# Two experts' outputs added by TensorE with one-hot gates, and the residual not lent as a place for weights, in a two-layer decoder trunk

## The chip, the cores and the metric

One core of one Trainium2 chip. The time is that of the whole program in device microseconds (us), the median of several executions. The profile is taken from one more execution.

## What is computed

Input x is 512 tokens of width D = 1024 in float32. Two layers, each of a token mixer (layer 0: RWKV-7 time mixing, layer 1: a Conformer convolution module) and a mixture of 32 gated-MLP experts of which each token uses two, with a residual around each, and a root-mean-square norm ahead of each and at the end:

```python
for i in range(2):
    hn = rms_norm(h, norm1_g[i])
    h = h + (rwkv7_time_mix(hn) if i == 0 else conformer_conv(hn))
    hn = rms_norm(h, norm2_g[i])
    # router: top 1 of 4 groups, top 2 of its 8 experts; ge is zero but for two experts of a token
    y = 0
    for wg, wu, wd, ge in experts:                 # (1024,256), (1024,256), (256,1024)
        y = y + ge[:, None] * ((silu(hn @ wg) * (hn @ wu)) @ wd)
    h = h + y
return rms_norm(h, final_g)
```

## The kernel before

All 512 tokens lie in four tiles of 128 partitions; h, the residual, is 128 x 4096 float32 in SBUF (2 MB). Each engine has a program of its own, written out by hand; they meet only at semaphores. The stages are: mixer 0, norm and routing, experts of layer 0, load back and combination, mixer 1, norm and routing, experts of layer 1, load back and combination, final norm.

**Experts.** Routing gives each expert up to 64 slots. In `pe_moe`, for each expert, TensorE multiplies the gathered rows of a pair of experts (`columns`, L911, then `gate_up`, L944), turns the product (`flip`, L920) and multiplies by the second matrix (`down`, L957). ScalarE applies silu (L987), copies the turned product (L993) and the result (`take_y`, L998) to SBUF; VectorE weighs (L1015) and gates (L1030). GpSimd gathers rows of the residual from DRAM (`rows`, L862) and scatters each result to the tensor `chosen` in DRAM (L871), four rows of 512 per token: two choices, two halves. After the last result is in DRAM (`round_done`), `act_load_back` reads `chosen` back, 1 MB a tile, and `dve_combine` (L1065) adds it to h with the gate of each token, two additions a tile.

**Weights.** SyncE (SP) issues all weight loads in one queue, in order: 2 MB of gate and up (`sp_load_up`, L404, in two halves L392 for some) and 1 MB of down (L409) for each expert. The up matrices have RING = 7 places, the down matrices DOWN_RING = 7. `sp_moe_weights` loads expert e into the place of expert e - 7 once that has been multiplied. Six of the up places are memory of their own; the seventh is h itself: once the normed rows are made and the residual has been stored to `rows` in DRAM (L847), `sp_load_into_h` loads expert 6 there, and after expert 27 `sp_return_h` (L422) reads the residual back.

**Around the experts.** `pe_stay_busy` (L740) issues matmuls whose result nobody uses. `pe_ranks`, `pe_slots` (L797) and `pe_factors` (L808) count slots and put row factors in slot order; `dve_tables` makes the index tables. All of this runs once ahead of the loop over rounds and once more in it for the next round; with this input one round is run. `pe_conv` begins with eight more unused matmuls (L2283), started by the first combined tile; then come transposes of the normed rows (L526) and the first products of the convolution module (L2290). In the norm ahead of it ScalarE squares (L468) and takes logarithm and exponential for two tiles together (`act_norm_rows`), and VectorE multiplies by the factor and by the norm's weights (L498). VectorE's first gate of the module is L2440.

## Time and profile before

| | us |
|---|---|
| median of 3 runs | 1242.36 (1239.82 to 1242.53) |
| the profiled execution | 1240.7 |
| its span in the profile | 1238.9 |
| TensorE busy | 1128.2 (91%) |
| VectorE busy | 521.1 (42%) |
| ScalarE busy | 419.4 (34%) |
| GpSimd busy | 214.3 (17%) |

The first mixer and the routing last until about 520 us, layer 0's experts until 738, the convolution module and its routing until about 991, layer 1's experts until 1209, the rest until the end. The page cuts the span into 40 slices of 31 us. Matmuls in float32 are listed as two passes each, so that a matmul of 512 columns counts as two; a busy TensorE is not one at its peak.

### The profile page before, as it was taken

The numbers are of one execution on the slowest core, as the hardware profiler recorded it, in microseconds if no ns is written. First come the engines' busy times: TensorE is split into PE (matmuls) and PEld (weight loads), VectorE is DVE, ScalarE is ACT, GpSimd is POOL, SyncE is SP. The second block draws the span as 40 slices with busy tenths as digits, with TensorE's granted clock in tenths as the row PEclk, the third lists the DMA queues.
The fourth block names the chain that finished last, engine by engine and source line by source line (L and its number), as shares of the span: only waits on it lengthen the run. The fifth ranks groups of instructions, "written<-read, shape, count | busy, mean of one in ns | idle before, by whom it ended". The sixth has DMA issues, their size and how long they took to land.

```text
span 1238.9 us, 29223 instructions
## 1 busy us (share of the span) xinstructions
PE 1128.2 (91%) x12462; PEld 622.5 (50%) x12462; DVE 521.1 (42%) x964; ACT 419.4 (34%) x815; POOL 214.3 (17%) x245
## 2 busy tenths in 40 slices
PE   6999999999999999899998876999999899998880
PEld 5455555555555644555554434544554455554440
DVE  5756555564665411511110105799941511111105
ACT  5335445444454421311111113555443321111112
POOL 2000000000000000222221110688800222222110
PEclk9999999999999989899998987999999899999995
DMA  4011101011012168799999996216502899999996
GB/s 159 3 54 62 40 21 58 4 57 41 20 58 85 59 248 332 258 406 423 426 423 426 425 385 252 93 68 249 244 0 74 318 352 423 425 425 424 425 381 240
DMA packets 51923, 274.57 MB, mean 222 GB/s; under 512 B 14900, under 2 KB 17076, under 8 KB 34642
## 3 DMA queue, kind: packets, MB, share of 16 engines
q1 hardware_dynamic: 39184, 243.28, 48.9%
q0 software_dynamic: 10880, 21.00, 4.5%
q10 hardware_dynamic: 1728, 8.42, 1.8%
q8 instruction: 100, 1.64, 0.5%
q14 instruction: 31, 0.24, 0.1%
HBM read 266.36 MB, written 23.07 MB: 234 GB/s over the span
## 4 chain that ended last, share of the span: by engine, by line
PE 78%; DMA 11%; ACT 4%; DVE 3%; issue 2%; SPq 2%; ACTq 0%; POOLq 0%; DVEq 0%
PE psum L944 14%; PE psum L1504 14%; PE psum L2034 9%; PE psum L2312 8%; DMA big<-in_moe_w_gate_up_dram 7%; PE psum L957 7%; PE psum L1685 6%; DMA big<-in_moe_w_down_dram 2%; PE psum L911 2%; PE psum L1808 1%; PE psum L2322 1%; PE psum L2290 1%; PE psum L526 1%; PE psum L1834 1%; ACT big L1867 1%
## 5 line engine op out<-in xcount | busy, mean ns | idle before, releaser
L944 PE MATMUL psum<-big 128*64 128x256 f32 x1536 | 191.6, 393 | 21.2 <-issue 12.9
L1504 PE MATMUL psum<-big 128*128 128x512 f32 x384 | 191.0, 618 | 5.5 <-ACT big L1555 4.3
L944 PEld LDWEIGHTS psum<-big 128*64 128x64 f32 x1536 | 107.2, 139 | 89.2 <-issue 30.6
L1030 DVE SCALAR_TENSOR_TENSOR big<-psum,big 128x128 f32<-128x128 f32 x64 | 22.5, 351 | 304.9 <-ACT big L987 304.9
L957 PE MATMUL psum<-big 128*64 128x512 f32 x512 | 120.9, 593 | 2.1 <-DMA big<-in_moe_w_down_dram 1.5
L871 POOL DMA_INDIRECT chosen<-big x64 | 63.7, 996 | 330.3 <-ACT big L998 177.2
L2034 PE MATMUL psum<-big 128*128 128x512 f32 x256 | 116.3, 607 | 0.8 <-ACT big L2417 0.8
L1877 ACT COPY big<-psum 128x512 f32<-128x512 f32 (+1 forms) x112 | 68.4, 649 | 113.6 <-PE psum L1685 111.7
L2262 POOL TENSOR_TENSOR big<-big 128x512 f32<-128x512 f32 x76 | 96.7, 1273 | 34.3 <-ACT big L2399 24.1
L847 POOL DMA_DIRECT2D rows<-h x8 | 4.7, 582 | 555.6 <-DVE h L2073 555.6
L2312 PE MATMUL psum<-big,conv_w 128*128 128x512 f32 x224 | 96.5, 592 | 0.0
L1504 PEld LDWEIGHTS psum<-big 128*128 128x128 f32 x384 | 64.8, 189 | 59.9 <-issue 53.9
L1685 PEld LDWEIGHTS psum<-big 64*64 64x64 f32 x4096 | 70.5, 134 | 43.0 <-issue 43.0
L2473 DVE SCALAR_TENSOR_TENSOR psum<-big,conv_taps,psum 128x512 f32<-128x512 f32 x123 | 82.3, 750 | 0.0
L1685 PE MATMUL psum<-big 64*64 64x64 f32 (+1 forms) x4096 | 80.0, 227 | 0.3 <-ACT big L1877 0.2
L2034 PEld LDWEIGHTS psum<-big 128*128 128x128 f32 x256 | 48.3, 194 | 58.4 <-issue 54.6
L2399 ACT ACTIVATE big<-big,conv_taps 128x512 f32<-128x512 f32 x84 | 57.2, 716 | 46.5 <-DVE big L2440 28.4
L993 ACT COPY big<-psum 128x128 f32<-128x128 f32 x64 | 17.0, 265 | 155.3 <-PE psum L920 106.7
L2312 PEld LDWEIGHTS psum<-big,conv_w 128*128 128x128 f32 x224 | 42.6, 190 | 53.1 <-issue 53.1
L998 ACT COPY big<-psum 128x512 f32<-128x512 f32 x64 | 37.4, 585 | 88.6 <-PE psum L957 88.6
L1015 DVE TENSOR_TENSOR big<-psum,big 128x1024 f32<-128x1024 f32 (+1 forms) x34 | 39.3, 1161 | 65.3 <-PE psum L911 65.3
L957 PEld LDWEIGHTS psum<-big 128*64 128x64 f32 x512 | 36.6, 137 | 48.1 <-issue 37.5
(273 smaller groups left out, 1355.9 us busy)
## 6 DMA issues: line engine op xcount, KB each, us to landing
big<-in_moe_w_gate_up_dram SPq DMA_DIRECT2D x40, 2048.0 KB
big<-in_moe_w_down_dram SPq DMA_DIRECT2D x64, 1024.0 KB
conv_w<-in_moe_w_gate_up_dram SPq DMA_DIRECT2D x8, 2048.0 KB
h<-in_moe_w_gate_up_dram SPq DMA_DIRECT2D x8, 2048.0 KB
big<-in_moe_w_gate_up_dram SPq DMA_DIRECT2D x16, 1024.0 KB, 38.4
big<-in_rwkv_w_rkv_dram SPq DMA_DIRECT2D x24, 512.0 KB, 4.3
conv_w<-in_conv_w_pw_dram SPq DMA_DIRECT2D x8, 1024.0 KB, 4.8
big<-chosen ACTq DMA_DIRECT2D x6, 1024.0 KB, 9.3
```

The lines of the kernel that those rows point to most:

```text
L871: nc.gpsimd.indirect_dma_start(chosen[m.layer], bass.IndirectOffsetOnAxis(ap=m.scatter_at[:, e:e + 1].bitcast(u32), axis=0), m.y[e % Y_RIN ...
L944: last = nc.tensor.matmul(o[half * SLOTS:(half + 1) * SLOTS, 0:F_EXP].rearrange("p (u f) -> p u f", u=2), m.xT[e // 2 % 2][:, c, (e % 2) * ...
L957: last = nc.tensor.matmul(bank[6 + e % 2][half * SLOTS:(half + 1) * SLOTS, :], m.zT[e % 2][:, k, :], m.down[j][:, k, half * 512:(half + 1) ...
L1015: return nc.vector.tensor_tensor(m.xT[p % 2][:, first:end, :], psum[:, first * P:end * P].rearrange("p (c s) -> p c s", s=P), m.g_col[:, f ...
L1504: last = nc.tensor.matmul(bank[b], m.w[:, n, c, :], x[:, c, :], start=(c == 0), stop=(c == C - 1))
L1685: last = nc.tensor.matmul(bank[b + hd][half(par ^ (hd & crossed)), at:at + w.shape[1]], lhs(hd, cp, par), w, start=True, stop=True)
L1877: nc.scalar.copy(dst, src).then_inc(done.now(), 1)
L2034: return nc.tensor.matmul(bank[4 * (t % 2) + nh], src[:, c, t * P:(t + 1) * P], wts[:, nh * 512:(nh + 1) * 512], start=(c == 0), stop=(c = ...
L2262: nc.gpsimd.tensor_tensor(out_, m.product[n % 4], m.product[(n - 1) % 4] if k == 1 else out_, ALU.add).then_inc(m.pool_tap, 1)
L2312: last = nc.tensor.matmul(up_bank(q, u), m.w1[b][:, c, u, :], m.hnT[:, c, :], start=(c == 0), stop=(c == C - 1))
L2399: nc.scalar.activation(m.product[n % 4], m.u[b][:, at:at + T], ACT.Copy, scale=m.taps[:, q, at:at + 1]).then_inc(m.product_ready, 1)
L2473: done[k % 2] = st.done(nc.vector.scalar_tensor_tensor(out=m.co[:, q, :] if k == DVE_TAPS[q] - 1 else acc[k % 2], in0=m.u[b][:, k:k + T], ...
```

## The change

**Two experts not scattered.** The results of experts 30 and 31 are no longer written to `chosen`. VectorE makes, for each of the two, a matrix of 128 tokens by slots with the gate in it (`spread_gates`); TensorE turns it (`turn_hot`), ScalarE copies it to SBUF (`take_hot`), and behind the last `down` TensorE multiplies it by the result: 64 slots x 128 tokens times 64 x 512, two halves, two experts, four tiles (`add_last`). VectorE adds these sums from PSUM to h. The gates of the other rows are set to zero where the row belongs to expert 30 or 31.

**The load back** waits for expert 29's scatter alone (`round_done` is raised there), is issued by SP at the end of `sp_moe_weights` and lands in the up places 2 and 3. The combination is now inside the round, in the order COMBINE, with `dve_tables` for the next round behind the second addition.

**The residual stays in SBUF.** RING is 6; `sp_load_into_h` and `sp_return_h` are gone. `chosen` has rows that nobody writes, so it is filled once with finite values (`sp_finite`, eight DMAs of 1 MB behind the convolution vectors' load in the first mixer).

**Norms behind the experts.** Tile by tile: ScalarE squares, takes logarithm and exponential and writes the scaled rows. For the convolution module the norm's weights are applied at the transposed columns, by ScalarE in eight copies a tile (tiles 0 and 1) or by VectorE in two (tiles 2 and 3). In the final norm GpSimd multiplies tiles 0 and 1 by the weights and VectorE makes tiles 2 and 3. The eight unused matmuls of `pe_conv` and one of three ahead of the experts are gone; `pe_factors` moves into the loop. `pe_slots` of the next round moves from expert 28 to expert 31.

```diff
-RING = 7
+RING = 6
 DOWN_RING = 7
 N_PAIRS = N_EXP // 2
 Y_RING = 2
+ADDED_BY_PE = 2
+SCATTERED = N_EXP - ADDED_BY_PE
...
-                self.back = [big[:, stage_base // 2 + 2 * D * t:stage_base // 2 + 2 * D * (t + 1)] for t in range(TT)]
+                places = [ring_up[n].rearrange("p u c f -> p (u c f)") for n in (2, 3)]
+                self.back = [places[t // 2][:, t % 2 * 2 * D:(t % 2 + 1) * 2 * D] for t in range(TT)]
...
-        def sp_load_into_h(m, sp):
-
-            sp.wait_ge(m.squares.sem, m.squares.by(TT))
-            sp.wait_ge(m.hnT_in_psum.sem, m.hnT_in_psum.by(TT))
-            sp.wait_ge(m.rows_stored.sem, m.rows_stored.by(16 * TT))
-            sp_load_up(m, sp, RING - 1)
-
-        def sp_return_h(m, sp, rounds):
-
-            assert max(range(RING - 1, N_EXP, RING)) <= LAST - FREE2
-            sp.wait_ge(m.gate_up_done, FREE2 - 2 + UPS_A_ROUND * rounds)
-            sp.dma_start(h, rows[m.layer].rearrange("(t p) d -> p t d", p=P)).then_inc(m.first_pick_in, 16)
-
...
+            sp_load_back(m, sp, 0)
...
+        def sp_load_back(m, sp, r):
+
+            back = chosen[m.layer].rearrange("(t p c) n -> t p (c n)", p=P, c=4)
+            sp.wait_ge(m.round_done, r + 2)
+            sp.dma_start(m.back[0][:, 0:D], back[0][:, 0:D]).then_inc(m.first_pick_in, 16)
+            sp.dma_start(m.back[0][:, D:], back[0][:, D:]).then_inc(m.back_in[0].sem, 16)
+            for t in range(1, TT):
+                sp.dma_start(m.back[t], back[t]).then_inc(m.back_in[t].sem, 16)
+
+
+
+        COMBINE = tuple(("pick", t, k) for t in range(2) for k in range(2)) + tuple(
+            ("last", t, n) for t in range(2) for n in range(2)) + tuple(
+            (what, t, n) for t in range(2, TT) for what in ("pick", "last") for n in range(2))
+        H_STEPS = len(COMBINE)
+
+        def h_step_of(what, t, n):
+            return COMBINE.index((what, t, n)) + 1
...
+        def act_norm_root(m, act, rounds, t):
+
+            act.wait_ge(moe[m.after].h_step, summed(moe[m.after], rounds, t))
+            nc.scalar.activation(big[:, last_region:last_region + D], h[:, t, :], ACT.Square,
+                                 accum_out=m.ss[:, t:t + 1]).then_inc(m.squares.sem, 1)
+            rstd = m.rstd[:, t:t + 1]
+            act.wait_ge(m.squares.sem, m.squares.by(t + 1))
+            nc.scalar.activation(rstd, m.ss[:, t:t + 1], ACT.Ln, scale=1.0 / D, bias=rms_eps[:]).then_inc(m.rstd_step.sem, 1)
+            act.wait_ge(m.rstd_step.sem, m.rstd_step.by(2 * t + 1))
             nc.scalar.activation(rstd, rstd, ACT.Exp, scale=-0.5).then_inc(m.rstd_step.sem, 1)
...
+        def act_norm_rows(m, act, t):
+
+            act.wait_ge(m.rstd_step.sem, m.rstd_step.by(2 * t + 2))
+            if t >= len(m.hn):
+                act.wait_ge(m.hnT_in_psum.sem, m.hnT_in_psum.by(t - len(m.hn) + 1))
+            nc.scalar.activation(m.hn[t % len(m.hn)], h[:, t, :], ACT.Copy, scale=m.rstd[:, t:t + 1]
+                                 ).then_inc(m.hn_ready.sem, 1)
...
+                for e in range(SCATTERED):
+                    if e + 1 < SCATTERED:
                         scatter(e + 1)
                     if e % 2 == 0 and e // 2 + 4 < N_PAIRS:
                         gather(e // 2 + 4)
                     scattered(e)
                 pool.sem_inc(m.round_done, 1)
+                pool.wait_ge(m.last_added.sem, TT * r + (m.last_added.before + TT))
+                pool.sem_inc(m.y_free, ADDED_BY_PE)
...
+        GATES_A_ROUND = ADDED_BY_PE * TT + 2
...
-            pe_stay_busy(m, 3)
+            pe_stay_busy(m, 2)
             rounds = load_rounds(m, pe)
             with pe.Fori(0, rounds) as r:
+                pe.wait_ge(m.h_step, H_STEPS * r + H_STEPS)
+                pe_factors(m, pe, r)
...
+                def turn_hot(j):
+
+                    pe.wait_ge(m.last_hot_ready.sem, ADDED_BY_PE * r + (m.last_hot_ready.before + j + 1))
+                    pe.wait_ge(m.xT_ready, ROWS_A_ROUND * r + (FREE1 + rows_of(N_PAIRS - 1)))
+                    for t in range(TT):
+                        last = nc.tensor.transpose(bank[j][:, t * P:(t + 1) * P], m.last_hot[:, t, :], ident[:])
+                    last.then_inc(m.last_turned.sem, 1)
+
+                def add_last(j, t):
+
+                    for half in range(2):
+                        s = slice(half * SLOTS, (half + 1) * SLOTS)
+                        last = nc.tensor.matmul(bank[LAST_BANKS[t][half]], m.last_rows[s, j, t * P:(t + 1) * P],
+                                                m.y[(SCATTERED + j) % Y_RING][s, :], start=(j == 0),
+                                                stop=(j == ADDED_BY_PE - 1))
+                    return last
...
+                    if e == LAST:
                         pe.wait_ge(m.slot_step, TABLE_STEPS * r + TABLE_STEPS)
+                        pe.wait_ge(m.factor_ready.sem, r + (m.factor_ready.before + 1))
                         pe.sem_inc(pe_tick)
                         pe_slots(m, pe, r + 1)
                     if e % 2 == 0 and e + 2 < N_EXP:
                         columns(e // 2 + 1)
+                    if e in (LAST - 2, LAST - 1):
+                        turn_hot(e - (LAST - 2))
                     if e + 1 < N_EXP:
                         gate_up(e + 1)
                     else:
                         flip(e)
                     down(e)
...
+                rows_turned(0)
+                add_last(0, 1)
+                rows_turned(1)
+                add_last(0, 0)
+                add_last(1, 0).then_inc(m.last_added.sem, 1)
+                add_last(1, 1).then_inc(m.last_added.sem, 1)
+                add_last(0, 2)
+                add_last(1, 2).then_inc(m.last_added.sem, 1)
+                pe.wait_ge(m.h_step, H_STEPS * r + (H_STEPS + h_step_of("last", 1, 1)))
+                add_last(0, 3)
+                add_last(1, 3).then_inc(m.last_added.sem, 1)
+            return rounds
...
+                def take_hot(j):
+                    act.wait_ge(m.xT_in_psum, ROWS_A_ROUND * r + rows_of(N_PAIRS - 2))
+                    act.wait_ge(m.last_turned.sem, ADDED_BY_PE * r + (m.last_turned.before + j + 1))
+                    nc.scalar.copy(m.last_rows[:, j, :], bank[j]).then_inc(m.last_rows_ready.sem, 1)
+
...
+                def spread_gates(j):
+
+                    dve.wait_ge(m.hot_ready, TT * 2 * r + TT * 2)
+                    if j:
+                        dve.wait_ge(m.last_turned.sem, ADDED_BY_PE * r + (m.last_turned.before + j))
+                    for t in range(TT):
+                        nc.vector.tensor_scalar(m.last_hot[:, t, :], m.hot[:, 2 * t, :], m.last_gate[:, t, 0, j:j + 1], None,
+                                                ALU.mult).then_inc(m.gates_step.sem, 1)
+                    for t in range(TT):
+                        dve.wait_ge(m.gates_step.sem, GATES_A_ROUND * r + (m.gates_step.before + TT * j + t + 1))
+                        last = nc.vector.scalar_tensor_tensor(out=m.last_hot[:, t, :], in0=m.hot[:, 2 * t + 1, :],
+                                                              scalar=m.last_gate[:, t, 1, j:j + 1], in1=m.last_hot[:, t, :],
+                                                              op0=ALU.mult, op1=ALU.add)
+                    last.then_inc(m.last_hot_ready.sem, 1)
...
+                def combine(what, t, n):
+
+                    if n or what == "last":
+                        dve.wait_ge(m.h_step, H_STEPS * r + (H_STEPS + h_step_of(*(("pick", t, n - 1) if what == "pick" and n
+                                                                                   else ("pick", t, 1)))))
+                    if what == "pick":
+                        if t == 0 and n == 0:
+                            dve.wait_ge(m.first_pick_in, 16 * r + 16)
+                        else:
+                            dve.wait_ge(m.back_in[t].sem, 16 * r + (m.back_in[t].before + 16))
+                        nc.vector.scalar_tensor_tensor(out=h[:, t, :], in0=m.back[t][:, n * D:(n + 1) * D],
+                                                       scalar=m.gate_now[:, n, t:t + 1], in1=h[:, t, :], op0=ALU.mult,
+                                                       op1=ALU.add).then_inc(m.h_step, 1)
+                    else:
+                        dve.wait_ge(m.last_added.sem, TT * r + (m.last_added.before + t + 1))
+                        part = h[:, t, n * 512:(n + 1) * 512]
+                        nc.vector.tensor_tensor(part, bank[LAST_BANKS[t][n]], part, ALU.add).then_inc(m.h_step, 1)
...
+                    if e == LAST - 4:
+                        spread_gates(0)
+                    if e == LAST - 2:
+                        spread_gates(1)
+                    if e == LAST - 1:
+                        dve.wait_ge(m.last_hot_ready.sem, ADDED_BY_PE * r + (m.last_hot_ready.before + ADDED_BY_PE))
+                        dve_slots(m, dve)
+                        gates_of_round()
+                for step in COMBINE:
+                    combine(*step)
+                    if step == ("pick", 0, 1):
+                        dve_tables(m, dve, r + 1)
             return rounds
-
-        def act_load_back(m, act, rounds):
...
-            pe.wait_ge(moe[0].h_step, 2)
-            for _ in range(8):
-                nc.tensor.matmul(bank[1], ident[:], h[:, 0, 0:512], start=True, stop=True)
...
+            def columns(t):
+                act.wait_ge(m.hnT_in_psum.sem, m.hnT_in_psum.by(t + 1))
+                for c in range(C):
+                    last = nc.scalar.activation(m.hnT[:, c, t * P:(t + 1) * P],
+                                                bank[NORM_BANKS[t % 2][c // 4]][:, c % 4 * P:(c % 4 + 1) * P], ACT.Copy,
+                                                scale=m.g_col[:, c:c + 1])
+                    if c % 4 == 3:
+                        last.then_inc(m.hnT_ready.sem, 1)
...
+        def dve_conv(m, dve):
+            dve.wait_ge(m.vec_in, CONV_VECTORS_IN)
+            for t in range(2, TT):
+                dve.wait_ge(m.hnT_in_psum.sem, m.hnT_in_psum.by(t + 1))
+                for half in range(2):
+                    c = slice(4 * half, 4 * half + 4)
+                    nc.vector.tensor_tensor(m.hnT[:, c, t * P:(t + 1) * P],
+                                            bank[NORM_BANKS[t % 2][half]].rearrange("p (c t) -> p c t", t=P),
+                                            m.g_col[:, c].unsqueeze(2).broadcast_to([P, 4, P]), ALU.mult
...
+        def sp_finite(sp):
+
+            for m in moe:
+                rows_of_tokens = chosen[m.layer].rearrange("(t p k c) n -> t p k (c n)", p=P, k=2, c=2)
+                for t in range(TT):
+                    sp.dma_start(rows_of_tokens[t], h[:, t, :].unsqueeze(1).broadcast_to([P, 2, D])
+                                   ).then_inc(chosen_finite.sem, 16)
+
+        def pool_final(m, pool):
+            pool.wait_ge(m.params_in.sem, m.params_in.by(16))
+            for t in range(EARLY):
+                pool.wait_ge(m.hn_ready.sem, m.hn_ready.by(t + 1))
+                nc.gpsimd.tensor_tensor(m.hn[t], m.hn[t], m.g_row, ALU.mult).then_inc(m.early_rows.sem, 1)
```

## Rows read from the trace of the kernel before

**Rows 1.** Page, part 2: granted clock of TensorE and GB/s in 40 slices of the span.

```profile
PEclk9999999999999989899998987999999899999995
...
GB/s 159 3 54 62 40 21 58 4 57 41 20 58 85 59 248 332 258 406 423 426 423 426 425 385 252 93 68 249 244 0 74 318 352 423 425 425 424 425 381 240
```

**Rows 2.** Waits of TensorE, 655:738, then 1105:1209: total us, times, longest us.

```profile
PE psum L944 <- issue: 8.5, 4, 2.6
PE psum L944 <- DMA big<-in_moe_w_gate_up_dram: 2.7, 3, 1.9
...
PE psum L957 <- DMA big<-in_moe_w_down_dram: 1.5, 2, 0.9
```

**Rows 3.** Timeline of SyncE's DMA issues, layer 0: start us, us, engine, line, operation.

```profile
509.66 0.33 SPq L404 DMA_DIRECT2D h<-in_moe_w_gate_up_dram  x1
522.29 7.38 SPq L392 DMA_DIRECT2D big<-in_moe_w_gate_up_dram  x4
...
718.01 0.38 SPq L422 DMA_DIRECT2D h<-rows  x1
```

**Rows 4.** Windows, layer 0's experts: us, busy by engine, PEclk, DMA share, GB/s.

```profile
522.30:735.60 213.30, 200.12 (x1424) 107.44 (x1420) 31.08 (x55) 39.56 (x96) 43.41 (x43) 0.98 1.01 417
```

**Rows 5.** Timeline behind layer 0's experts, columns as in rows 3, idle before it in brackets.

```profile
730.70 0.98 POOL L871 DMA_INDIRECT chosen<-big  x1 [8.55 <-ACT big L998]
...
735.65 1.94 PE L957 MATMUL psum<-big 128*64 128x512 f32 x8 [0.59 <-ACT big L993]
...
749.57 2.70 DVE L1065 SCALAR_TENSOR_TENSOR h<-big,h 128x1024 f32<-128x1024 f32 x2 [2.24 <-DMA big<-chosen]
...
764.94 3.72 PE L2290 MATMUL psum<-big,conv_w 128*128 128x256 f32 x16 [1.25 <-ACT big L480]
...
781.03 0.75 DVE L2440 SCALAR_TENSOR_TENSOR big<-psum,conv_vec,big 128x512 f32<-128x512 f32 x1 [11.72 <-PE psum L2290]
```

**Rows 6.** The chain that ended last, behind layer 0's experts: start us, us, what.

```profile
739.07 6.18 DMA chosen<-big
```

**Rows 7.** Timeline behind layer 1's experts.

```profile
1200.50 0.98 POOL L871 DMA_INDIRECT chosen<-big  x1 [6.58 <-ACT big L998]
...
1206.68 1.94 PE L957 MATMUL psum<-big 128*64 128x512 f32 x8 [0.90 <-DMA big<-in_moe_w_down_dram]
...
1217.71 1.28 DVE L1065 SCALAR_TENSOR_TENSOR h<-big,h 128x1024 f32<-128x1024 f32 x1 [2.12 <-DMA big<-chosen]
...
1233.29 2.61 DVE L498 SCALAR_TENSOR_TENSOR big<-h,big 128x1024 f32<-128x1024 f32 x2 [0.51 <-ACT big L475]
```

**Rows 8.** Groups by line: xcount | busy us, mean ns | idle before it.

```profile
L2262 POOL TENSOR_TENSOR big<-big 128x512 f32<-128x512 f32 x76 | 96.7, 1273 | 34.3 <-ACT big L2399 24.1 <-POOL big L2262 0.4
...
L1065 DVE SCALAR_TENSOR_TENSOR h<-big,h 128x1024 f32<-128x1024 f32 x16 | 20.5, 1284 | 8.0 <-DMA big<-chosen 7.2
...
L993 ACT COPY big<-psum 128x128 f32<-128x128 f32 x64 | 17.0, 265 | 155.3 <-PE psum L920 106.7 <-issue 48.6
...
L1981 DVE TENSOR_TENSOR big<-big 128x256 f32<-128x256 f32 x8 | 3.3, 416 | 0.0
...
L688 DVE TENSOR_TENSOR big<-big,token_high 128x256 bf16<-128x256 f32 x4 | 2.4, 630 | 0.1
...
L2455 DVE TENSOR_TENSOR big<-psum,big 128x512 f32<-128x512 f32 x3 | 2.1, 692 | 0.4 <-PE psum L2322 0.3
```

**Rows 9.** Timeline of layer 0's routing: GpSimd beside VectorE's L688.

```profile
507.75 2.10 POOL L831 TENSOR_TENSOR big<-big 128x256 bf16<-128x256 f32 x3 [6.17 <-DVE big L683]
```

**Rows 10.** Timeline of TensorE: eight passes in the first mixer, six passes of filling.

```profile
119.81 3.67 PE L1504 MATMUL psum<-big 128*128 128x512 f32 x8 [0.61 <-ACT big L1555]
...
513.37 5.30 PE L740 MATMUL psum<-big,ident 128*128 128x512 f32 x6
```

**Rows 11.** Timeline of TensorE (first mixer), and a window of the output's writes.

```profile
143.97 1.12 PE L1504 MATMUL psum<-big 128*128 128x512 f32 x2
...
1236.00:1237.00 1.00, 0.00 (x0) 0.00 (x0) 0.00 (x0) 0.00 (x0) 0.00 (x0) 0.50 0.93 381
```

255 lines of the change are left out of this document (112 added, 143 removed).

## The prediction

> **What bounds the kernel now.** The slices of the page come first [rows 1]. In both mixture-of-experts stages (slices 17 to 22 and 33 to 37) the core's DMA moves 423 to 426 GB/s, whatever else is going on. To see which of the two sets the pace, read the waits of TensorE over the last 83 us of layer 0's experts [rows 2]: 8.5 us in four gaps that the view can only call issue, and 2.7 us that it gives to gate and up weights. Over the first 130 us the same view is empty. So TensorE runs ahead of the weights at first, uses up what was loaded in advance, and from 655 us it goes at the pace of the weight stream. Layer 1 ends the same way [rows 2]. In that regime the end of the experts is the end of the stream: what was not in SBUF when the stream began has to be moved at 417 GB/s [rows 4].
>
> Behind the last expert nothing of that sort holds. Layer 0: last `down` begins at 735.65 and takes 1.96, so it ends at 737.6; the output goes to SBUF, is scattered to DRAM from 739.07 on [rows 6], read back, and VectorE's first gated addition is at 749.57, 12.0 us after the last matmul; the mixer's first gate is at 781.03 [rows 5]. Layer 1: 1208.6, 1217.71 (9.1 us), last row of the final norm 1233.29 for two of 1.3, end at 1238.9 [rows 7]. The tails are therefore 43.4 and 30.3 us long. The profiled execution took 1240.7 us, 1.7 under the median of the runs.
>
> **What the change does to the weight stream.** The seventh `up` place was the residual's own 2 MB. Its load for expert 6 is issued at 509.66 and has 12.6 us to itself before the first place comes free, at 522.29 [rows 3]; it fills time in which nothing else of the stream is to be moved. With RING = 6 these 2.1 MB wait for expert 0 to free its place, and are moved inside the saturated stretch: 2.10 MB by 417 GB/s is 5.0 us, per layer [rows 4]. The 2 MB read that returned the residual (issued 718.01) goes, but it was queued after the last weight, so it gives nothing back to them. In the new order `down` 7 is issued behind both halves of `up` 8 (the places for `up` 6 to 8 come free in the first 13 us, at the rate at which experts finish), and by then the queue runs dry once for 0 to 2 us: I take 0.9. Moving `pe_slots` (16 short matmuls, about 0.64 us) to just before the last `flip` delays the last `down` by 0 to 0.6: 0.3, since that `down` mostly waits for its weights. The two hot-matrix transposes (half a microsecond of TensorE each), 16 small VectorE operations in `spread_gates` and two 128x512 copies on ScalarE lie in the last four experts, where each engine waits for the stream anyway: nothing; were the stream not the limit they would cost at most 1 us on TensorE. Sum: **+6.2 us a layer, +12.4**, bounds 4.9 and 7.6 a layer.
>
> **What it takes from the tails.** The load back no longer waits for the last scatter but for that of expert 29. That one was issued at 730.70 and 1200.50, 6.9 and 8.1 us before the last matmul ended [rows 5, 7]. The last scatter took 6.2 us in layer 0 with the DMA still loaded [rows 6], and so ended at 745.3. With 6 to 7 us for it, round_done comes about when the last `down` ends, 0.6 us before or after; issue to first addition is 4.3 us (745.3 to 749.57). So the first addition is at **+3.5 us** after the last matmul instead of 12.0 and 9.1. Bounds 2.5 and 5.5. SP is blocked on round_done there; queued behind it are the mixer's first weights, issued at 718.4 before, which now follow 4 MB of read-back: 5 MB, 12 us, still before their use.
>
> **What it puts there instead.** VectorE had eight additions of 1.28 us; it now has the eight, eight of 128x512 from PSUM at 0.69 and the tables of the next round (five small operations, about 1.1 us by an estimate from the 0.4 of a 256-wide one and less) in between [rows 8]: 17.8 us from first addition to last, in the order of COMBINE: rows of tile 0 complete at 8.2 (2.7 before), tile 1 at 9.6, tile 2 at 13.7, tile 3 at 17.8. TensorE's 16 products are 32 passes of 512 columns; even one behind the other at 0.46 us [rows 10] those of tile 0 are done 6 us after the last `down`, of tile 1 8 us and of tile 2 11 us, and VectorE asks for them at 10.2 us and later.
>
> Layer 0, counted from the first addition: ScalarE does square, logarithm, exponential and scaled copy of a tile in 2.9 us (two passes over 1024 columns at about a microsecond and two single columns at 0.2, my estimate), so the rows are normed at 11.1 and 14.0. Its eight small copies for a tile's columns are 2.1 us (0.265 each [rows 8]); columns of both tiles at 18.1 (before: TensorE begins its products at 764.94, which is 15.4). Then 256-wide products: four groups of 3.5 us at full clock. They follow, with the transposes of tiles 2 and 3 (ScalarE delivers at 20.8 and 23.6) and VectorE's scaled copies between, to 35.0 at full clock. The change also takes out the eight dummy matmuls (L2283) that kept TensorE busy from the end of the first tile on and brought the clock up before these products. The granted clock of the slice with that tail is 0.7 in the mean, of the last slice 0.5 [rows 1]; what the lower level costs is seen at the start of the experts, where six filling passes take 5.30 us, 0.88 each, against 0.46 for a pass of the same width at full clock [rows 10]. The first group here would then take 6.9 us, of which 1.7 isn't covered by ScalarE. I take it: first gate at 37.0, against 31.5 before. Tail 3.5 + 37.0 = 40.5 against 43.4: **-2.9 us**.
>
> Layer 1: last addition at 17.8, square, logarithm and exponential of tile 3 to 19.6, its scaled copy on VectorE to 20.9, then the 3.0 us to the end as before: 23.9. New beside it are two 128x1024 multiplications on GpSimd, 2.5 us each by the 1.27 for 512 columns [rows 8], at about 11 and 14 us, when VectorE does additions whose two inputs are both in SBUF. The one place in the trace where both do that at once is L688 beside L831: 0.63 us, where the same width alone takes 0.42 (L1981), half as much again [rows 8, 9]. On the four additions of 1.28 this is 2.5 us: I take that; bounds 0 and 5.1, two whole multiplications. Tail 3.5 + 23.9 + 2.5 = 29.9 against 30.3: **-0.4 us**.
>
> The Trainium skill, "SBUF — State Buffer", section "SBUF: two separate sides", says that the port pair shared by VectorE and GpSimd is an exclusive lock held for the whole instruction. By that rule the price is the upper bound, 5.1 us. The 0.63 against 0.42 speaks for some blocking and can't tell how much of it.
>
> **Starts of the experts and the rest.** TensorE's first transposes follow right behind the six passes of filling, which end at 518.7 [rows 10]. With one filler less and `pe_factors` behind them it could begin up to 1.4 us earlier, once the gather has landed; but the clock may then rise later, up to 2 us lost. I take 0, bounds -1.4 and +2 a layer. The new fill of `chosen` is 8.4 MB of writes issued around 103 us. Output rows are written at 381 GB/s, so it ends near 126 us; the value weights queued behind it are used first at 143.97 [rows 11]. Cost 0; it begins to cost if the writes run under about 220 GB/s.
>
> **Sum.** +12.4 - 2.9 - 0.4 = +9.1 us: 1240.7 becomes 1249.8; I say 1250.
>
> **The rivals.**
> 1. The seventh place was worth nothing: the stream carries 2 MB less (the returned residual) and 2 MB more, and if the DMA engines work on the return and the last weights together, the end doesn't move. It decides at whether the return slowed the last weights by as much as 5 us. For it: the return is issued 16 us before the last `down` ends. Against: it is behind them in the same queue. Then +9.1 - 11.8 = -2.7: 1238, faster. 0.17.
> 2. The tails are as short as they can be: clock full, no loss beside GpSimd, start 0.9 us earlier in both layers: 9.1 - 1.7 - 2.5 - 1.8 = +3.1, with the dry spell gone +1.3: 1242 to 1244, within the limit of what can be told. 0.15.
> 3. GpSimd holds up VectorE for both its multiplications: +2.6 more, 1252.4. The rule cited above says so. 0.18.
> 4. Expert 29's scatter lands late, since it shares engines with the last weights: the first addition at 8 us in both layers, as though nothing had been cut in layer 1: +9, 1259. 0.06.
> The forecast itself: 0.44.
>
> **How the numbers follow.** 0.2% is 2.5 us, about what a measurement of this kernel can tell from none. Faster is rival 1 (0.17), same is rival 2 (0.15), slower the rest, 0.68. The range goes from the middle of rival 1 past rival 3, as far as the bounds of the first addition (2.5 to 5.5, twice) and of the starts reach together: 1238 to 1257.
>
> **What would show it.** The sum of TensorE's waits for weights in the experts rises by about 5 us a layer and the first such wait comes earlier; last `down` to last `down` of layer 0 is the plainest number. First addition 3.5 us after it. Mixer's first gate 40.5 after it, and the end of the span 29.9 after that of layer 1. VectorE's additions longer than 1.28 only in layer 1 after tile 1. I am wrong if the last `down` of layer 0 ends within 2 us of 737.6, or if the load back is issued well before the last `down` ends.

## The result, and the profile after

| | before | after |
|---|---|---|
| median, us | 1241.5 (1239.8 to 1242.5, 4 runs) | 1254.7 (1253.3 to 1255.8, 4 runs) |
| ratio of the runs, with its interval | 1 | 1.0102 [1.0082, 1.0123] |
| span of the profiled execution, us | 1238.9 | 1253.2 |
| mean granted clock of TensorE | 0.967 | 0.974 |

The change costs 13.2 us. I had said 1250, +9.1. The sign and the order of size are right, the size is 4 us short, and that is more than the runs scatter. Medians are of the fast runs alone: e2, e6, e12 and the repeats of before had one run each that took 1642, 1902, 4591 and 2267 us, and it is left out. The changed kernel was timed four times, the experiments at other times beside new runs of before, whose median was then 1242.0 to 1242.7. The ratios are not quite the quotients of two medians. By their intervals, a difference between an experiment and the changed kernel is good to 3 to 4 us; where it is smaller, the time alone doesn't show it. The page of the changed kernel, part 2, has the two rows that answer [rows 1]:

```profile
PEclk9999999999999999899999997999999899999997
...
GB/s 157 3 53 300 61 28 58 5 55 41 19 57 118 25 289 330 184 407 423 422 423 423 422 303 268 68 100 266 187 0 117 229 389 421 423 422 422 422 309 218
```

The fourth slice is new (300 GB/s where there were 62: the fill of `chosen`); the experts run at 421 to 423, before at 423 to 426. To see where the 14.3 us of span went, cut the program at five points that every variant has: the first bf16 matmul of the ranks (routing), the start of ScalarE's copy of expert 31's output (the last `down` has ended), the mixer's first gate, and the same in layer 1. All kernels of this study are cut here, in us; the stretch from the first gate to layer 1's routing was 197.8 to 197.9 in every one, and is left out.

| kernel | routing 0 at | routing to last `down`, layer 0 | tail 0 | routing to last `down`, layer 1 | tail 1 | span |
|---|---|---|---|---|---|---|
| before | 507.8 | 229.9 | 43.4 | 229.8 | 30.3 | 1238.9 |
| after | 508.5 | 238.5 | 40.1 | 237.6 | 30.7 | 1253.2 |
| e1 six places | 507.4 | 235.1 | 40.1 | 236.5 | 29.7 | 1246.6 |
| e2 lend | 511.0 | 235.1 | 40.3 | 235.1 | 32.8 | 1252.1 |
| e3 no GpSimd | 506.7 | 237.7 | 40.5 | 237.2 | 28.5 | 1248.5 |
| e4 warm | 508.3 | 236.6 | 38.5 | 239.0 | 31.0 | 1251.2 |
| e5 before, fill | 509.3 | 232.8 | 43.4 | 229.7 | 30.3 | 1243.4 |
| e6 six, return | 505.5 | 234.7 | 43.2 | 234.5 | 30.3 | 1246.0 |
| e7 combination | 507.6 | 232.5 | 39.4 | 230.6 | 29.8 | 1237.7 |
| e8 aligned | 509.1 | 237.3 | 38.3 | 233.9 | 31.7 | 1248.1 |
| e9 fill in pieces | 507.5 | 238.9 | 40.1 | 236.7 | 30.6 | 1251.7 |
| e10 combination, split | 506.9 | 233.8 | 38.8 | 230.8 | 28.9 | 1237.0 |
| e11 four fillers | 507.9 | 231.4 | 40.4 | 232.3 | 29.6 | 1239.4 |
| e12 before, shifted | 507.7 | 232.0 | 44.2 | 232.3 | 30.4 | 1244.4 |

Before to after: +0.7 (routing), +8.6, -3.3, +7.8, +0.4: together 14.3 with rounding. One execution stands behind each row of the table, and one stretch varies by up to 2 us and more between kernels that are alike in it: before and e5 have 229.8 and 229.7 in layer 1, but e1 and e6, which differ only behind the last weights, have 236.5 and 234.5 there, and routing of the kernels without a fill at once begins at 505.5 to 507.9. A single difference of less than 2 us in this table shows nothing by itself; the rows of the trace that explain it, or several kernels on each side, have to.

The waits of TensorE in layer 0's experts, first 522 to 650, then 650 to 747 (before, the first stretch was empty, and the second is [rows 2]):

```profile
PE psum L940 <- DMA big<-in_moe_w_gate_up_dram: 2.9, 2, 2.2
...
PE psum L940 <- DMA big<-in_moe_w_gate_up_dram: 8.8, 5, 2.5
PE psum L940 <- issue: 3.9, 2, 2.0
PE psum L940 <- DMA conv_w<-in_moe_w_gate_up_dram: 2.0, 1, 2.0
```

[rows 2] leave out one line of the same view of before, the wait for the expert in the lent place:

```profile
PE psum L944 <- DMA h<-in_moe_w_gate_up_dram: 1.4, 1, 1.4
```

With it the waits for gate and up weights were 12.6 us (8.5, 2.7, 1.4). They are 17.6 now, 5.0 more, and they begin before 650. SyncE's issues, and the start of the experts on TensorE, answer to [rows 3, 10]:

```profile
524.42 13.16 SPq L395 DMA_DIRECT2D big<-in_moe_w_gate_up_dram  x6
537.63 0.62 SPq L412 DMA_DIRECT2D big<-in_moe_w_down_dram  x1
...
512.36 1.96 PE L726 MATMUL psum<-h,ident 128*128 128x512 f32 x4
...
518.63 1.97 PE L907 MATMUL psum<-ident,big 128*128 128x128 f32 x8 [3.72 <-DMA big<-rows,big]
520.70 5.61 PE L940 MATMUL psum<-big 128*64 128x256 f32 x32
```

There is no issue at 509; the first place comes free at 524.42, 2.1 us later. The first transposes begin where they did, at 518.63, but behind 3.7 us of standing still, and the first gate and up products take 5.61 us where they took 3.67 before. The same two places in layer 1, the first freed place in before and after and the first products in after:

```profile
993.25 7.38 SPq L392 DMA_DIRECT2D big<-in_moe_w_gate_up_dram  x4
...
999.44 12.96 SPq L395 DMA_DIRECT2D big<-in_moe_w_gate_up_dram  x6
...
995.88 5.25 PE L940 MATMUL psum<-big 128*64 128x256 f32 x32 [0.51 <-DVE big L1053]
```

The issue at the first freed place cuts the stretch of the experts in two: the start, and the part in which the stream sets the pace. In us, layer 0 and layer 1:

| kernel | routing to first freed place | from there to the end of the last `down` |
|---|---|---|
| before | 14.5, 14.4 | 215.3, 215.4 |
| after | 15.9, 14.5 | 222.5, 223.1 |
| e1 six places | 14.4, 13.4 | 220.7, 223.1 |
| e6 six, return | 14.3, 13.4 | 220.3, 221.1 |
| e2 lend | 17.2, 16.3 | 218.0, 218.8 |
| e8 aligned | 16.4, 13.2 | 220.9, 220.7 |
| e12 before, shifted | 15.0, 15.2 | 217.1, 217.1 |
| e10 combination, split | 17.1, 14.0 | 216.7, 216.8 |
| e11 four fillers | 15.1, 14.6 | 216.3, 217.7 |

Behind the last matmul of layer 0, for [rows 5, 6]:

```profile
737.10 0.66 PE L964 MATMUL psum<-ident,big 128*128 128x128 f32 x4
...
738.65 0.98 POOL L861 DMA_INDIRECT chosen<-big  x1 [6.23 <-DMA chosen<-big]
...
741.96 1.94 PE L953 MATMUL psum<-big 128*64 128x512 f32 x8 [0.18 <-DMA big<-in_moe_w_down_dram]
...
743.83 0.64 PE L785 MATMUL psum<-big 128*128 128x64 bf16 x16
...
744.93 0.33 SPq L460 DMA_DIRECT2D big<-chosen  x1
...
746.95 0.58 ACT L1029 COPY big<-psum 128x512 f32<-128x512 f32 x1 [2.04 <-PE psum L953]
...
749.04 1.28 DVE L1106 SCALAR_TENSOR_TENSOR h<-big,h 128x1024 f32<-128x1024 f32 x1 [6.47 <-DMA big<-chosen]
...
768.37 6.39 PE L2356 MATMUL psum<-big,conv_w 128*128 128x256 f32 x16 [3.63 <-ACT big L2442]
...
787.04 0.75 DVE L2518 SCALAR_TENSOR_TENSOR big<-psum,conv_vec,big 128x512 f32<-128x512 f32 x1 [8.80 <-PE psum L2356]
...
738.65 6.14 DMA chosen<-big
```

The load back is issued 2.0 us before the last `down` ends (746.95), and the first addition comes 2.1 us behind it; the mixer's first gate is 38.0 after that. Layer 1, for [rows 7]:

```profile
1222.50 0.58 ACT L1029 COPY big<-psum 128x512 f32<-128x512 f32 x1 [2.13 <-PE psum L953]
...
1224.85 2.72 DVE L1106 SCALAR_TENSOR_TENSOR h<-big,h 128x1024 f32<-128x1024 f32 x2 [6.96 <-DMA big<-chosen]
...
1236.69 1.29 DVE L1112 TENSOR_TENSOR h<-psum,h 128x512 f32<-128x512 f32 x2
...
1237.90 4.56 DVE L1106 SCALAR_TENSOR_TENSOR h<-big,h 128x1024 f32<-128x1024 f32 x2
1238.29 6.37 POOL L2628 TENSOR_TENSOR big<-big 128x1024 f32<-128x1024 f32 x2 [23.33 <-PE psum L971]
...
1242.58 1.29 DVE L1112 TENSOR_TENSOR h<-psum,h 128x512 f32<-128x512 f32 x2
1243.79 3.16 DVE L2641 SCALAR_TENSOR_TENSOR big<-h,big 128x1024 f32<-128x1024 f32 x2
```

### The profile page after: what moved, and what is told of

Its sections match the earlier page's. It is cut to its first block, busy times and chain, and to the rows that moved or that the text cites. A ratio compares the mean times of both kernels' runs of the same rounds, so it can differ in the third digit from the quotient of the medians.

```text
span 1253.2 us, 29408 instructions
## 1 busy us (share of the span) xinstructions
PE 1139.9 (91%) x12474; PEld 626.5 (50%) x12474; DVE 536.0 (43%) x1012; ACT 430.6 (34%) x841; POOL 216.9 (17%) x244
## 4 chain that ended last, share of the span: by engine, by line
PE 67%; DMA 22%; ACT 4%; DVE 4%; issue 2%; SPq 0%; DVEq 0%; POOLq 0%; ACTq 0%
DMA big<-in_moe_w_gate_up_dram 19%; PE psum L1563 14%; PE psum L940 10%; PE psum L2093 9%; PE psum L2379 8%; PE psum L1744 6%; PE psum L953 4%; PE psum L2356 1%; PE psum L1867 1%; PE psum L907 1%; PE psum L2389 1%; DMA big<-chosen 1%; PE psum L505 1%; PE psum L1893 1%; DMA chosen<-big 1%
## 5 line engine op out<-in xcount | busy, mean ns | idle before, releaser
L940 PE MATMUL psum<-big 128*64 128x256 f32 x1728 | 220.1, 399 | 34.9 <-DMA big<-in_moe_w_gate_up_dram 26.4
L940 PEld LDWEIGHTS psum<-big 128*64 128x64 f32 x1728 | 121.7, 142 | 116.1 <-DMA big<-in_moe_w_gate_up_dram 34.9
L861 POOL DMA_INDIRECT chosen<-big x60 | 60.0, 999 | 329.0 <-ACT big L1029 161.9
L2331 POOL TENSOR_TENSOR big<-big 128x512 f32<-128x512 f32 x76 | 96.7, 1273 | 38.5 <-ACT big L2478 28.0
L1053 DVE TENSOR_TENSOR big<-psum,big 128x1024 f32<-128x1024 f32 (+1 forms) x34 | 39.4, 1161 | 61.1 <-PE psum L907 61.1
L953 PEld LDWEIGHTS psum<-big 128*64 128x64 f32 x512 | 36.7, 137 | 47.6 <-issue 37.9
```

The costliest lines, as they stand in the source:

```text
L861: nc.gpsimd.indirect_dma_start(chosen[m.layer], bass.IndirectOffsetOnAxis(ap=m.scatter_at[:, e:e + 1].bitcast(u32), axis=0), m.y[e % Y_RIN ...
L940: last = nc.tensor.matmul(o[half * SLOTS:(half + 1) * SLOTS, 0:F_EXP].rearrange("p (u f) -> p u f", u=2), m.xT[e // 2 % 2][:, c, (e % 2) * ...
L953: last = nc.tensor.matmul(bank[6 + e % 2][half * SLOTS:(half + 1) * SLOTS, :], m.zT[e % 2][:, k, :], m.down[j][:, k, half * 512:(half + 1) ...
L1053: return nc.vector.tensor_tensor(m.xT[p % 2][:, first:end, :], psum[:, first * P:end * P].rearrange("p (c s) -> p c s", s=P), m.g_col[:, f ...
L2331: nc.gpsimd.tensor_tensor(out_, m.product[n % 4], m.product[(n - 1) % 4] if k == 1 else out_, ALU.add).then_inc(m.pool_tap, 1)
```

## The experiments

**e1, six places in the kernel before.** The change's `RING = 6` alone.

```diff
-RING = 7
+RING = 6
-            sp_load_into_h(moe[0], sp)        # and for moe[1]
-            sp.dma_start(h, rows[m.layer]...).then_inc(m.first_pick_in, 16)
```

> The kernel before with one edit of the change alone: RING = 6, so the residual's 2 MB are neither lent to expert 6 nor returned; tails, load back and fillers as before. Theory (the seventh place is worth the 2.1 MB it holds ahead of the saturated stream, 6.2 us a layer forecast, 7 to 8 read from the two traces): last down of layer 0 6 to 8 us after the 737.6 of before, whole time +12 to +15, about 1255, so that the rest of the change gives nothing or a little. Rival 1 (what is moved later is paid by the return that goes): last down of layer 0 within 2 us of 737.6, time within 2.5 us of before, and the 14 us come from something else in the change.

1246.9 us (1244.2 to 1250.9, 10 runs), ratio 1.0032 [1.0017, 1.0047]: +4.4, neither the 12 to 15 nor the 0. The last `down` of layer 0 did come late (742.47, +4.8), as the theory wanted. But the first addition is then 9.15 us behind it, not 11.9 as before, and in layer 1 8.25, not 9.1. So part of what the stream loses comes back behind it. In the part that goes at the stream's pace e1 is 5.4 and 7.7 us longer than before.

**e6, the same with the return kept.** One line back into e1: the read of 2 MB over h, though h was never lent.

```diff
+            sp.dma_start(h, rows[m.layer].rearrange("(t p) d -> p t d", p=P)).then_inc(m.first_pick_in, 16)
```

> The six-place version of before with one thing put back: the 2 MB read that returns the residual, at its old place behind the last weights, although the residual was never lent (it reads the same values over themselves). Theory (the return stands between the last weights and the scatters and load back, and its cost falls in the tail, not in the stream): last down of layer 0 within 1 us of 742.5, but the first addition 11 to 12 us behind it instead of 9.15, and the time 2 to 4 us above that of the six-place version (1246.9). Rival: the return is hidden behind the last experts as I predicted (gives nothing back, costs nothing): first addition 9 to 9.5 us behind, same time.

1249.7 us (1248.5 to 1251.6, 3 runs), ratio 1.0071 [1.0051, 1.0091]. That is 2.8 above e1 by the medians and 4.8 by the ratios, so the return costs something. The chain of e1 and then of e6, behind layer 0:

```profile
743.90 3.31 DMA chosen<-big
```

```profile
741.62 6.44 DMA chosen<-big
```

The last scatter lands in 3.31 us where nothing is queued in front of it, and takes 6.44 where the return is ([rows 6]: 6.18 before). First addition 12.15 and 9.03 us behind the last `down`, as before. This is the price of the return: 3.0 us in layer 0, 0.8 in layer 1. Against before, where all else is equal, the seventh place alone is worth 4.8 and 4.7 us in the table, and 5.0 and 5.7 in the part behind the first freed place. e1 has no return but the same experts, and there it comes to 5.2 and 6.7, and 5.4 and 7.7: four readings of one thing, from 4.7 to 7.7. In layer 1 both reach the first freed place 1.0 us sooner than before, with no lent load on its way then.

**e2, the residual lent again in the changed kernel.**

```diff
-RING = 6
+RING = 7
-                places = [... for n in (2, 3)]
+                places = [... for n in (0, 1)]
+            sp_load_into_h(moe[0], sp)        # and for moe[1]
+            sp_return_h(m, sp, 1)             # in front of the load back
```

> The changed kernel with the residual lent to expert 6 again (RING = 7, returned by a 2 MB read behind the last weights, load back into places 0 and 1 instead of 2 and 3), written for one round of slots, which is what this routing needs. All the rest of the change stays: last two experts added by TensorE, early load back, tables inside the additions, no dummies. Theory: takes back the whole ring loss, 12 to 15 us, to about 1240 to 1242, with the first addition still 2 to 4 us behind the last down unless the returned residual comes late. Rival 1: stays within 2.5 us of the changed kernel's 1254.7. Rival: the returned residual, queued behind the last weights, is what the first addition waits for, and 1 to 3 us of the 12 to 15 are lost again there.

1251.1 us (7 runs), ratio 1.0056 [1.0035, 1.0076]. -3.6 (-5.7 by the ratios), not -12 to -15: the theory that the ring makes the whole loss falls. The stretch is 3.3 and 2.5 us shorter than in the changed kernel (4.6 and 4.5 counted from the first transposes, which come 1.2 and 1.9 us later behind routing; the lent load is on its way with the first gather then), and still 5.3 longer than before in both layers, with as many places: 2.6 and 1.9 of it ahead of the first freed place, 2.6 and 3.4 behind it. The first addition is 4.0 us behind the last `down` instead of 2.1 to 2.4, again the return. What remained was to find 5.3 us in each layer that have nothing to do with the ring.

**e4, filling where TensorE stands still.**

```diff
                 pe_factors(m, pe, r)
+                pe_stay_busy(m, 3)
                 add_last(1, 2).then_inc(m.last_added.sem, 1)
+                for _ in range(4):
+                    nc.tensor.matmul(bank[5], ident[:], m.up[1][:, 0, 0:2, :], start=True, stop=True)
+            for _ in range(3):                # pe_conv, ahead of its wait for hnT_ready
+                nc.tensor.matmul(bank[1], ident[:], h[:, 0, 0:512], start=True, stop=True)
```

> The changed kernel with filling passes of TensorE where it idles: three dummy matmuls of 512 columns behind the gate factors at the start of the experts, four behind the products of tile 2 (both layers), three ahead of the mixer's first products. Theory (the first expert and the first product group run at the lower clock because TensorE stood still before them): first gate_up group 3.7 instead of 5.6 us and first product group 3.5 to 4.5 instead of 6.4; time 2 to 5 us under the changed kernel's. Rival (the lower clock comes whatever is put there, or the groups are covered by ScalarE and the weights): within 1.5 us of it, the first gate no earlier.

1250.8 us (1245.1 to 1252.9, 8 runs), ratio 1.0056 [1.0042, 1.0070]: -3.9. The groups went as the theory said:

```profile
518.83 1.16 PE L908 MATMUL psum<-ident,big 128*128 128x128 f32 x8 [1.42 <-DMA big<-rows,big]
520.50 3.67 PE L941 MATMUL psum<-big 128*64 128x256 f32 x32 [0.51 <-DVE big L1056]
...
766.16 3.72 PE L2359 MATMUL psum<-big,conv_w 128*128 128x256 f32 x16 [0.70 <-ACT big L2447]
```

The granted clock over the first group is 0.65 in the changed kernel and 1.00 in e4 (the number in front of the last two):

```profile
520.70:526.31 5.61, 5.61 (x33) 3.21 (x33) 0.63 (x1) 0.00 (x0) 0.99 (x1) 0.65 0.26 65
...
520.50:524.17 3.67, 3.67 (x33) 2.34 (x33) 0.37 (x1) 0.00 (x0) 0.99 (x1) 1.00 0.37 82
```

3.67 for 5.61, and 3.72 for 6.39. The first gate is 38.5 us behind the last `down` instead of 40.1; of 2.7 us less in the group 1.6 reach the gate. In layer 0 the stretch is 1.9 shorter; in layer 1 it is 1.4 longer, with the first group at 3.67 there too, which this run doesn't explain.

**e5, the fill alone in the kernel before.**

```diff
             sp_conv_vectors(cv, sp)
+            sp_finite(sp)
+            pool.wait_ge(chosen_finite.sem, chosen_finite.by(FINITE_STORED))   # and in dve_moe_norm
```

> The kernel before with the change's fill alone: eight transfers that write the residual's input over both chosen tensors (8.4 MB) in the first mixer, at the change's place in SP's queue, and the two waits for it. All else as before. Theory (the fill is what disturbs the first mixer: routing of layer 0 was 0.7 us later in the changed kernel, 3.2 us later with the residual lent again, but 1.0 earlier with no GpSimd at the end, so it varies): routing of layer 0 between 507 and 511 instead of 507.8, time +0.5 to +3. Second question: in the middle of the experts the changed kernel and the three kernels made from it move 421 to 422 GB/s, the two without a fill 424 to 426. If the fill has a part in that, this kernel shows 421 to 422 too and its experts take 1.2 us longer in each layer; if not, 424 or more.

1246.6 us (1245.9 to 1250.2, 4 runs), ratio 1.0048 [1.0029, 1.0067]: +4, more than expected. Routing is 1.6 us later. In the first mixer TensorE has waits that before has not (1.8 and 1.3 us; 2.1 and 1.6 in the changed kernel). The windows of the experts show 424 GB/s, so the fill has no part in the lower rate. The rest of the +4 lies in layer 0's experts: the first gather landed later, TensorE stood still for 1.56 us, and the first group took 5.21 us. That is 400 us behind the fill, and nothing here shows that the fill is its cause.

**e9, the fill in pieces in the changed kernel.**

```diff
-            sp_finite(sp)
             for q in range(1, PAIRS - 2):
                 ...
                 load_r(q + 2)
+                if q <= TT:
+                    sp_finite(sp, q - 1)      # 2 MB: tile q - 1 of both layers
```

> The changed kernel with its fill of chosen issued in four pieces of 2 MB, one in each of four head pairs of the mixer, instead of 8.4 MB at once. Theory (the fill at once holds TensorE for 2.1 us at one matmul group near 121 us and about 1 us beside it, in each of the four kernels that have it, and none of the three without): that wait is gone, routing of layer 0 at 505.5 to 507.8, time 1.5 to 3 us under the changed kernel's. Rival (the pieces disturb each pair a little instead): several waits of 0.5 us, same time within 1 us.

1252.3 us (1248.6 to 1254.9, 4 runs), ratio 1.0078 [1.0052, 1.0103]: -2.4, less than the times can show. The waits of TensorE that the view calls issue, 80 to 505 us, in the changed kernel and then with the pieces:

```profile
PE psum L1563 <- issue: 2.1, 1, 2.1
PE psum L1733 <- issue: 1.6, 2, 1.2
```

```profile
PE psum L1734 <- issue: 0.2, 1, 0.2
```

The 2.1 us are gone, 1.4 of the 1.6 beside them too, and routing starts at 507.5. Over all kernels of the table, routing starts at 508.8 in the mean of the six with a fill at once (506.7 to 511.0) and at 507.3 in the mean of the eight without (505.5 to 507.9): 1.5 us, with some overlap.

```diff
-        rms_eps = sb("rms_eps", [P, 1])       # e8: from in front of big ...
+        rms_eps = sb("rms_eps", [P, 1])       # ... to behind conv_taps
         half_shift = sb("half_shift", [P, 1]) # e12, kernel before
+        pad = sb("pad", [P, 1])
```

> The changed kernel with one thing moved: the new constant rms_eps (4 bytes a partition) is allocated behind the large tensors instead of in front of them, so that the tensor that holds the weight places begins at byte 35328 of a partition (a multiple of 64), as in the kernel before, and not 32 bytes further. Theory (the 32 bytes are why this kernel and all made from it move 421 to 422 GB/s in the middle of the experts, where those made from the kernel before move 424 to 426): 424 or more in the windows of the experts, experts 1 to 1.5 us shorter in each layer, time 2 to 3 us under 1254.7. Rival (the rate comes from something else in the change): 421 to 422 stays, and the time within 1.5 us.

> The kernel before with one unused constant of 4 bytes a partition allocated in front of the large tensor, so that this begins 32 bytes further on, at byte 35360 of a partition, as in the changed kernel. Nothing else. Theory (weight places at multiples of 32 but not of 64 bytes cost the weight stream 0.5%): 421 to 422 GB/s in the middle of the experts instead of 424 to 426, experts 1 to 1.5 us longer in each layer, time +2 to +3. Rival (the 3 us between the changed kernel and its aligned form were another effect of the order of allocation or scatter between runs): 424 or more, and the same time within 1.2 us.

e8: 1251.5 us (1249.8 to 1252.9, 4 runs), ratio 1.0082 [1.0062, 1.0102]: -3.2 against the changed kernel by the medians and -2.5 by the ratios, whose intervals touch. e12: 1245.8 us (11 runs) against 1242.7, ratio 1.0016 [1.0001, 1.0030]: +3.1 or +2.0, barely clear of none. What carries the case is the rate. The window 1070 to 1120 of layer 1 in four kernels, before, after, e8 and e12 (last two numbers: share of the DMA engines, GB/s):

```profile
1070.00:1120.00 50.00, 50.00 (x365) 27.20 (x363) 7.71 (x12) 9.75 (x25) 12.16 (x12) 1.00 1.01 424
```

```profile
1070.00:1120.00 50.00, 46.23 (x336) 24.93 (x332) 7.36 (x11) 9.11 (x22) 12.15 (x12) 1.00 1.01 422
```

```profile
1070.00:1120.00 50.00, 46.22 (x329) 24.34 (x325) 7.70 (x12) 9.49 (x23) 11.19 (x12) 1.00 1.01 424
```

```profile
1070.00:1120.00 50.00, 50.00 (x368) 27.21 (x366) 7.70 (x12) 9.74 (x24) 12.17 (x13) 1.00 1.01 421
```

The rate follows the 32 bytes in both directions. It does so in all fourteen kernels: from 560 to 700 and from 1030 to 1170 us the seven with `big` at 35328 (before, e1, e5, e6, e8, e10, e11) move 424 to 425 GB/s, the other seven 422. From first transposes to last `down`, e12 takes 220.7 us in both layers against 219.0; e8 takes 226.7 and 224.4 against 228.3. Not all of e8's 3.9 in layer 1 is the address, for its first group ran at the full clock there, behind 1.46 us of standing still, and gained 1.6:

```profile
993.77 3.67 PE L940 MATMUL psum<-big 128*64 128x256 f32 x32 [0.51 <-DVE big L1053]
```

Behind the first freed place, where that doesn't count, e8 is 1.6 and 2.4 us shorter than the changed kernel, and e12 1.7 longer than before in both layers. The Trainium skill, "DMA: Bandwidth & Descriptors", section "How a descriptor splits into AXI transactions", says that a read that doesn't begin at a multiple of 256 bytes fetches bytes that it doesn't use and pays for them; it speaks of reads, and here it is the written side that moved. 35328 is a multiple of 256, 35360 of 32 alone, and these runs don't tell at which boundary the price begins.

**e3, no GpSimd in the final norm.**

```diff
-            pool_final(fin, pool)
-                if t < EARLY:
-                    act_norm_rows(m, act, t)
-            for t in range(EARLY, TT):
+            for t in range(TT):               # dve_final: all four rows on VectorE
```

> The changed kernel with all four rows of the final norm scaled by VectorE behind its last addition; the two GpSimd multiplications and the two scaled copies on ScalarE go. Theory (the two additions of tile 3 took 2.28 us each instead of 1.28 because GpSimd worked beside them): the additions of tile 3 come back to 1.28 to 1.30 each, the last addition ends 2.0 us earlier; VectorE then does four rows of 1.3 instead of two of 1.58, so the end moves by -1 to +1. Rival (the 2.28 comes from something else, the DMA writes or ScalarE's square): the additions of tile 3 stay at 2.2 or more.

1250.0 us (1248.1 to 1250.8, 4 runs), ratio 1.0054 [1.0037, 1.0071], 4.7 under the changed kernel. 2.2 of them are in the stretch that the edit touches, tail 1; the others are in stretches that it leaves alone, and no larger there than the scatter. The additions of tile 3 and the rows after them:

```profile
1236.41 2.60 DVE L1106 SCALAR_TENSOR_TENSOR h<-big,h 128x1024 f32<-128x1024 f32 x2
...
1240.33 4.86 DVE L2639 SCALAR_TENSOR_TENSOR big<-h,big 128x1024 f32<-128x1024 f32 x4
```

2.60 us for the two where the changed kernel has 4.56. How the 4.56 came about is read from its chain and from a narrow window of its timeline:

```profile
1239.21 3.26 DVE h L1106
...
1241.34 3.33 POOL L2628 TENSOR_TENSOR big<-big 128x1024 f32<-128x1024 f32 x1
```

The first addition ends at 1239.2, and the second takes 3.26 us instead of 1.28: it stands 2.0, until GpSimd's first multiplication is over at 1241.3, and ends 1.2 behind that. GpSimd's second, 3.33 long, ends 2.2 behind the addition, at 1244.7. Read so, one engine works at a time, each for a whole instruction of 1.3 or some 2.1 us. The additions of the last experts, L1112, which read PSUM and h, pass by GpSimd's second at their usual 0.69. The first row of the norm, L2641, which reads SBUF twice, doesn't: begun at 1243.8, it ends 1.1 us behind GpSimd's second, and the two rows take 3.16 us where e3's four take 4.86. That is 0.7 more, so VectorE loses 2.7 in all. GpSimd began this late because its stream waited for TensorE's last product (the bracket of its line), not for its rows. The last waits of SyncE, in the changed kernel and in e3, show a second price:

```profile
SPq L106 <- PEq L106: 3.0, 1, 3.0
```

```profile
SPq L106 <- PEq L106: 0.2, 1, 0.2
```

After the last row has been written the program takes 3.0 us more to end. Those 3.0 to 3.2 us stand in all five kernels that have the two multiplications (after, e2, e4, e8, e9) and are 0.2 in the nine that have not. e3 takes out ScalarE's two scaled copies along with them, so strictly it is the pair that is shown.

**e7, e10 and e11, put together.** e7 is e2, e3, e4 and e9 in one. e10 returns the residual tile by tile and has `big` at 35328, with its last region at a multiple of 64 bytes too; e11 adds a fourth filler ahead of the experts. Like e2, all are written for one round of slots, which this routing needs; they would not serve a routing that needs more.

```diff
-            sp.dma_start(h, rows[m.layer]...).then_inc(m.first_pick_in, 16)
+            sp.dma_start(h[:, 0, :], rows[m.layer][0:P, :]).then_inc(m.first_pick_in, 16)
             for t in range(1, TT):            # in sp_load_back
+                sp.dma_start(h[:, t, :], rows[m.layer][t * P:(t + 1) * P, :]).then_inc(m.back_in[t].sem, 16)
                 sp.dma_start(m.back[t], back[t]).then_inc(m.back_in[t].sem, 16)
-                pe_stay_busy(m, 3)            # e11
+                pe_stay_busy(m, 4)
```

> Four things at once on the changed kernel: residual lent to expert 6 again, filling passes of TensorE as in the warm version, the final norm's rows all on VectorE, and the fill of chosen in four pieces of 2 MB, one in each of four head pairs of the mixer, where the DMA moves under 60 GB/s. Written for one round of slots. Theory (the terms add up): experts 219 to 221.5 us in each layer instead of 228.3, tail of layer 0 39 to 40.5, of layer 1 29.5 to 30.5, routing of layer 0 at 507 to 508.5: 1254.7 - 15 to - 18, so 1237 to 1240, 0 to 5 us under before. Rival (the parts give back to one another: the stream is the limit whichever end is shortened): 1243 or more.

> The combination of before (residual lent, filling passes, no GpSimd in the final norm, fill in pieces) with two more things: the residual is returned tile by tile, only tile 0 behind the last weights and tiles 1 to 3 each just ahead of the read-back of its tile, and the weight places begin at multiples of 64 bytes, the sixth too. Theory (2 MB of return ahead of the load back delay the first addition by 1.9 us in each layer; alignment gives 1.2 us a layer): first addition 2.1 to 2.8 us behind the last down instead of 4.0, experts 219.5 to 220, time 3 to 5 us under the combination's 1241.0, so 1236 to 1238 and below before. Rival (the returned tiles push the read-back of tiles 1 to 3 back by as much as tile 0 gains, additions end at the same time): first addition earlier, last addition not, time 1240 to 1242.

> The previous combination with four filling matmuls instead of three ahead of the first expert of each layer. There TensorE stood still for 1.43 us before the first transposes of layer 0 (for the gather), and the first gate_up group went part of its way at the lower clock (25 of its matmuls in 4.7 us; in layer 1, where the filling reached up to the transposes, all 32 took 3.67). Theory: the first group of layer 0 at 3.67, experts of layer 0 at 220 to 220.5 instead of 221.7, time 1 to 1.5 us under 1238.7. Rival (the late start is taken up by the weight stream): first group 3.67, but experts 221.5 and the same time.

e7: 1241.0 us (12 runs), ratio 0.9992 [0.9979, 1.0006], 13.7 under the changed kernel and the same as before; I had wanted 1237 to 1240. e10: 1238.7 us (12 runs), ratio 0.9977 [0.9963, 0.9991]. e11: 1238.2 us (6 runs), ratio 0.9958 [0.9945, 0.9972], 4.6 us under before. These two are the fastest kernels here, and the times don't tell them apart. In e10 the first additions came 2.3 and 2.2 us behind the last `down` instead of 4.0 and 4.2, but VectorE then took 18.0 and 18.8 us for them instead of 17.0 and 17.4: the last addition gained 0.6 and 0.7. The rival was nearly right, since the returned tiles stand between the read-backs. In e11 the first group of layer 0 took 3.67 and its experts 220.0 us (221.7), but layer 1's took 221.4 (220.4), and the medians differ by 0.5, not by the 1 to 1.5 of the theory.

## Why the prediction was right in sign and short in size

**The bound.** Right. The experts go at the pace of the stream, what was not moved in advance is moved in it, and the first wait for weights came earlier (before 650), as announced.

**The seventh place, +6.2 a layer.** Mechanism and size are right as far as can be told. Of the 6.2, 5.9 are the bytes and the dry spell, both behind the first freed place. There e6 and e1 have 5.0, 5.7, 5.4 and 7.7; over the whole stretch they have 4.8, 4.7, 5.2 and 6.7, from just under my lower bound of 4.9 to within the upper of 7.6. The 5.0 us of 2.1 MB at 417 GB/s would do for the lower ones, and no run shows the dry spell of 0.9 by itself. One reading was short: I took the waits of layer 0 as 11.2 us and left out the 1.4 for the lent place's weights. From 12.6 they rise by 5.0, as announced.

The whole stretch grew by 8.6 and 7.8, in sum 16.4 where I had 12.4. The pieces are these, in us, the ring by e6 and the address by e12, both against before:

| piece | layer 0 | layer 1 | my term, a layer |
|---|---|---|---|
| start, up to the first freed place | 1.4 | 0.2 | 0, bounds -1.4 and +2 |
| ring, behind it | 5.0 | 5.7 | 5.9 |
| address, behind it | 1.7 | 1.7 | not in the sum |
| rest, behind it | 0.5 | 0.3 | 0.3 |

- *Starts of the experts.* Both of my bounds happened in part. The transposes came 0.8 and 1.4 us sooner behind routing, and the first place came free 2.1 and 1.6 us later behind them, since TensorE had stood still for 3.7 and 1.2 us and its first group took 5.61 and 5.25 us at the lower clock. e4 and e11 show that a filler in that gap brings the group to 3.67 and makes layer 0's experts 1.9 and 1.7 us shorter; in layer 1 e4 has the 3.67 and is not shorter. I had called gain and loss even, though before had its transposes right behind fillers [rows 10].
- *32 bytes of address.* Not in the prediction at all: 1.7 us a layer by e12, 1.6 and 2.4 by e8 behind the first freed place, 2.0 to 3.2 in all by the times. The diff has it, as one new constant in front of `big`; no row of before could price it.
- *The end of the experts.* I put the two transposes of the hot matrices at nothing and `pe_slots` at 0.3, because the engines wait for the stream there. That held. In layer 0 the `down` behind the second pair of transposes (0.66 at 737.10) still waited 0.18 us for its weights at 741.96, so they cost nothing. From its start to the end of the last `down` it is 5.0 us with `pe_slots` (0.64 at 743.83) in between, and was 4.7 before: 0.3. In layer 1 the last `down` itself waits for its weights.

The pieces come from different kernels, and each of them can be off by a microsecond or two. They leave e2 in part open: behind the first freed place it is 2.6 and 3.4 us longer than before, of which the address is 1.7. e10 and e11, with as many places and the old address, are still 1.0 to 2.3 us longer there, and no run says why.

**Rival 1, the return.** It was wrong as I put it (2 MB less against 2 MB more, end unmoved: the last `down` moved by 9.3 us), but its transfer had a price that I didn't see. "It gives nothing back" is true of the weights and false of what is queued behind it: 3.0 us in layer 0, 0.8 in layer 1 (e6 against e1). The sum was not hurt, since I measured the old tails with the return in them. A reader who takes the seventh place's worth from e1's time alone gets 4.4 us for two layers and is wrong by half.

**First addition 3.5 behind the last `down`.** It was 2.1 and 2.35, outside the bounds of 2.5 to 5.5. The scatter of expert 29 was issued 8.3 us before the last `down` ended, not 6.9. From the `down` of expert 29 to that of 31 it is 9.7 us where it was 8.3, since the weights now set the time there (the 0.18 at 741.96). So part of what looks like a gain of the tail is a loss of the stretch before it. round_done came 2.0 us before that end, not within 0.6 of it, and a load back issued well before it was one of my signs of being wrong. Scatter 6.14 and issue to addition 4.1 were as taken.

**Tail 0.** 40.1 against 40.5, -3.3 against -2.9. That it is so close is luck: the first addition was 1.4 too late in the forecast and the gate behind it 1.0 too early. Additions 17.0 (17.8, where my own terms add up to 16.9 and I gave no reason for the rest); first products at 19.3 after the first addition (18.1), and 6.39 us for the first group (6.9): the lower clock was read rightly from the six fillers, and of the 1.7 us of it that I took to be uncovered e4 gives back 1.6. Gate at 38.0 (37.0).

**Tail 1.** 30.7 against 29.9, but from other terms. First addition 1.1 earlier; additions 19.0 where I had 20.3; and 3.0 us at the end of the program that I had not. *GpSimd beside VectorE, 2.5, bounds 0 and 5.1*: it is 2.0 on the additions and 0.7 on the first row of the norm, 2.7 in all. The size is right and the mechanism is not: I took 1.28 us additions to run half as long again, four of them, from 11 us on. The rule of the Trainium skill cited in the prediction ("SBUF — State Buffer", "SBUF: two separate sides") says that the port pair is an exclusive lock held for the whole instruction, and the trace agrees: the second addition stands until the multiplication ends. What was wrong in rival 3 is the count. Each multiplication held up one instruction of VectorE, but neither for its whole length: 2.0 of some 2.1 us for the first, and only 0.7 for the second, since two additions from PSUM ran beside it.

**The fill, 0.** Too low, by an amount that isn't well shown. I looked only at whether it ends before the value weights are used [rows 11], and it does (about 126 us). It still came with waits of TensorE, 2.1 us and about 1.4 beside that; what they were for, the view doesn't name. In pieces they are gone. At routing 1.5 us are left of them in the mean of the kernels. The time is 2.4 us less in e9, within what can be told, and 4 more in e5, of which only 1.6 lie ahead of routing.

By the spans I was 5.2 us short (14.3 against 9.1), by the medians 4; the profiled execution is the slowest of the four. Of the 5.2, 4.1 are in the experts: 3.4 for the address, 1.6 for the starts and 0.8 of rest, less 1.7 by which my ring term and `pe_slots` exceed e6. Routing has 0.7, tail 1 0.8, where the program's last wait outweighs the earlier first addition, and tail 0 gives back 0.4. So the mechanism that the change is about was right, and what was missing stood beside it.

## What to carry to other kernels

Price a prefetch place as the bytes it holds ahead of the saturated stretch by the stream's rate, and look for the price of a return in whatever is queued behind it, not in the stream. Read a diff for what it does beside its purpose: a new constant in front of a large tensor, a filler that no longer covers a wait and a one-time write of 8 MB stood in the sum at nothing, and cost some 3.4, 1.6 and 1.5 us here. Where two engines take turns at a port, count which instructions can stand in front of which, not how many there are. And before a stretch is charged to a cause, look how far it moves between two kernels that are the same in it: here it was up to 2 us.

## What the runs showed of the hardware

- Weight places in a tensor that begins at byte 35360 of a partition instead of 35328 take the stream from 424 or 425 to 422 GB/s, and the reverse (e12, e8): 1.7 us a layer in e12, whose time rose by 3.1 (by its interval, 0.1 to 3.7).
- TensorE's clock can be at its lower level (1.2 of 2.4 GHz) behind a short gap. Standing still for 3.7, 1.56 or 1.2 us before the first transposes was followed by 5.61, 5.21 and 5.25 us for the group of 32 matmuls, with a mean granted clock of 0.65, 0.70 and 0.69 over it; 1.43 us in e10 by 5.36 (0.68). After 1.46 us (e8, layer 1), 1.42 us (e4) and 1.08 us (e5, layer 1), and where fillers reached up to the transposes, the group took 3.67 at 1.00. So the length of the gap alone does not decide it.
- With two GpSimd multiplications in the last 15 us of the program its end was 3 us longer: SyncE's last wait is 3.0 to 3.2 us instead of 0.2. The view names TensorE's sequencer as what it waited for, and whether and why this hangs on GpSimd stays open.
- 8.4 MB of writes at once came with two waits of TensorE in the first mixer, 1.8 to 2.1 and 1.3 to 2.0 us, in each of the six kernels that have them; four pieces of 2.1 MB in e9 did not.
- A GpSimd multiplication and a VectorE instruction with two inputs in SBUF (128x1024) did not run at once: VectorE's took 3.26 instead of 1.28 us. One with an input in PSUM did (0.69).
- A scatter of an expert's result landed in 3.31 us with nothing queued in front of it and in 6.44 us behind a read of 2 MB (e1, e6).
